# The forget gates' affine steps in the second projection's first pass: from VectorE to ScalarE

## The chip, the cores and the metric

The kernel runs on one core of a Trainium2 chip. The metric is the device time of one execution in microseconds (us), the median of several runs; lower is better. A core has five engines that run their own instruction streams and meet at semaphores: TensorE (PE in the profile; its weight loads are PEld), VectorE (DVE), ScalarE (ACT), GpSimd (POOL) and SyncE (SP), which here only issues DMA transfers.

## The reference, cut to what matters

One inference step of a two-layer encoder: 2048 prompt tokens and 8 x 16 sample tokens, model width 1024, float32. Each layer starts with a projection of the normalized input to 3584 columns:

```python
def rmsnorm(x, g):
    y = x32 * lax.rsqrt(jnp.mean(x32 * x32, axis=-1, keepdims=True) + EPS)
    return (y * g.astype(F32)).astype(x.dtype)

def in_proj(x, g, w):
    p = rmsnorm(x, g) @ w
    m = MIX_WIDTH          # 768
    return (p[..., :m], p[..., m:2 * m], p[..., 2 * m:3 * m],
            heads(p[..., 3 * m:3 * m + X_WIDTH], H_X, HD_X), p[..., 3 * m + X_WIDTH:])
```

In the second layer the second of these blocks, z, gives the forget gates of a gated linear recurrence, and the last block a silu gate:

```python
def hgrn2_inputs(a, b, c, lb):
    z = heads(b, H_B, DK_B).astype(F32)
    lbh = lb.reshape(H_B, DK_B)
    log_f = jnp.logaddexp(jnp.log(lbh), jnp.log1p(-lbh) + jax.nn.log_sigmoid(z))
    k = (1.0 - lbh) * jax.nn.sigmoid(-z)
    return q, k, i, log_f
```

So for each element of z the kernel needs k = (1 - lb) * sigmoid(-z) and f = lb + (1 - lb) * sigmoid(z), with lb one number for each of the 768 channels. Behind the projections come a band attention (layer 0), the recurrence (layer 1), cross-attention and an output projection in each layer.

## The kernel before

The program is a row of stages: an opening, projection 0 (to about 640 us), the band attention, projection 1 (about 1286 to 1910 us), the sample tokens' mixer and the recurrence. A projection is the function `project`. It keeps channels on the partitions: the weight is cut into 28 groups of 128 output channels, taken as 14 pairs ("columns" 0 to 13 in the order of `ORDER`), and the tokens into 4 passes. The first pass is the widest: its tiles are 128x640 in place of 128x512, since it also takes the sample tokens.

One column in one pass is a 2x2 block product done in Strassen's way: 7 products ("steps" or terms 0 to 6). Each step multiplies a sum or difference of weight blocks by one of activation blocks. For float32 accuracy a weight term is split in a high half (L503, ScalarE) and a low half (L510, VectorE), activations too (L395, L399), and a step is 4 matmuls with the low weight half (L1456) and 8 with the high one (L1460). In the first pass the weight sums are made on the spot (L472; terms 0, 1 and 3 on VectorE, 5 and 6 on GpSimd) and SP stores them to DRAM for the later passes (L483). A low half takes the place of its sum in memory, so it waits for that store. SP also stores the finished outputs (L1081, L1086).

The products leave the accumulators so: ScalarE copies steps 0, 1 and 3 into the output tile (`copy`, L1198 and L1201), and VectorE combines steps 2, 3, 4 and 6 into it (`combine`, L1301). The combine of step 2 waits for the copy of step 1, that of step 3 for the copy of step 3 (semaphore `s_cp`).

The order of each engine's instructions is written out by hand as a loop over an iteration number t, at which TensorE is at about step t. In iteration t ScalarE does: copy of step t-1; high half of step t+5; a row of sigmoids, if t is 7q+8 (row 1 of column q) or 7q+9 (row 0); other work by place, such as evacuating transposed activations (L1226). VectorE does: combine of step t-1; the weight sum of step t+6; low half of step t+2; the gates of a row, if t is 7q+9 or 7q+10; other work. SP does: store of the term of step t+4, and for gated columns the output store at t = 7q+13. Engines run in order, so an instruction that waits holds all behind it. TensorE's step needs its low half (`s_lo`).

Columns 3 to 6 are silu gates. Columns 7, 8 and 9 hold the forget gates, in layer 1 only. Their sigmoids and gates are made while the next column multiplies. For each of the two rows (128 channels) of such a column ScalarE's `sigmoid` makes sigmoid(-z) into a second tile (L1212) and sigmoid(z) in place (L1214); VectorE's `gated` multiplies the first by 1 - lb (L1313) and turns the second into lb + (1 - lb) * sigmoid(z) (L1314), and raises `s_post`. The stores wait for `s_post`, and so does the next gated column's sigmoid. In the pieces below, `by_act` does not exist yet.

Of the kernel before, what the change touches and what calls it, by code (L numbers as in the profile page):

```python
# [17 lines left out]
ACT = mybir.ActivationFunctionType  # L18
# [24 lines left out]
GQ, GK, GV, GX, GG = 0, MG, 2 * MG, 3 * MG, 3 * MG + 2  # L43

HALF, SHALF = 2 * P, P // 2
PASSES, TERMS, WPAIRS = NT // 4, 7, NG // 2
STEPS = TERMS * WPAIRS
ORDER = [0, 1, 2] + list(range(GG // 2, NG // 2)) + list(range(3, GG // 2))


def place(step):
    p, r = divmod(step, STEPS)
    c, j = divmod(r, TERMS)
    return p, c, j


def column(q):

    p, c = divmod(q, WPAIRS)
    return WPAIRS - 1 - c if p % 2 else c  # L60
# [21 lines left out]
def wait(eng, sem, value):  # L82

    if not (isinstance(value, int) and value <= 0):
        eng.wait_ge(sem, value)
# [875 lines left out]
def project(nc, l, sem, ps_in, v, x, w, x_of, proj, keep, room, early, samp, opening):  # L961
    ident, g_ln, neg_half = v["ident"], v["g_ln"], v["neg_half"]
    ALL, TILES = PASSES * STEPS, 4 * (PASSES - 1)
    s_cp, s_cb, s_sig, s_post = (sem(f"pj{l}_{n}") for n in ("cp", "cb", "sig", "post"))
    s_mm = w.s_mm
    s_st = samp.s_store if l else opening.s_st
    s_st2 = samp.s_store2 if l else None
# [9 lines left out]
    lb, lb1 = v["lb"], v["lb1"]  # L977
# [6 lines left out]
    plain, gate, forget = "plain", "gate", "forget"  # L984

    def kind_of(q):
        g = 2 * ORDER[column(q)]
        return gate if g >= GG else forget if l and GK <= g < GV else plain
# [6 lines left out]
    def before(q):  # L995

        return sum(2 * each(i) for i in range(q))

    def each(q):
        return COUNT[kind_of(q)]  # L1000

    def rank(q):

        return sum(each(i) > 0 for i in range(q))

    def older(q):

        return max([i for i in range(q) if each(i)], default=0)

    def gates_stored(q, b):  # L1010

        return 16 * sum(1 + 2 * (i < WPAIRS) for i in range(q) if kind_of(i) == forget and rank(i) % 2 == b)

    NOUT, LATER = (3, 13) if l else (2, 11)
# [5 lines left out]
    with ExitStack() as ctx:  # L1020
        ps = ps_in(ctx)
        if room is None:
# [7 lines left out]
        WIDE, nat, out, sig, junk, ss, ms, rs = (  # L1030
            room.WIDE, room.nat, room.out, room.sig, room.junk, room.ss, room.ms, room.rs)

        def sig_of(q):
            return room.sig2[rank(q) % 2] if l else room.last if q // WPAIRS == PASSES - 1 else sig
# [20 lines left out]
        def row_of(q, row):  # L1055
            p = q // WPAIRS
            return slice(0, WIDE) if p == 0 else slice(SHALF, SHALF + 2 * HALF)
# [8 lines left out]
        with nc.Block() as block:  # L1066
            @block.sync
            def _(sp):
                def store(q):
                    p, c = q // WPAIRS, column(q)  # L1070
                    if kind_of(q) == plain:
                        sp.wait_ge(s_cb, 4 * q + 4)
                    else:
                        sp.wait_ge(s_post, before(q) + 2 * each(q))
                    groups = slice(2 * ORDER[c], 2 * ORDER[c] + 2)
                    if kind_of(q) == forget:
                        place_in(v["kgate"][groups.start - GK:groups.stop - GK], sig_of(q), p, s_st2[rank(q) % 2])
                    place_in(proj[groups], out[q % NOUT], p, s_st[q % NOUT])

                def place_in(to, buf, p, s_done):  # L1080
                    sp.dma_start(to[:, :, 2 * HALF * p:2 * HALF * (p + 1)].rearrange("g p n -> p g n"),  # L1081
                                 buf[:, :, SHALF:SHALF + 2 * HALF]).then_inc(s_done, 16)
                    if p == 0:
                        for row in range(2):
                            ends = bass.AP(buf[:].tensor, WIDE * row, [[2 * WIDE, P], [WIDE - SHALF, 2], [1, SHALF]])
                            sp.dma_start(to[row, :, SEQ:NTOK].rearrange("p (h n) -> p h n", h=2), ends).then_inc(s_done, 16)  # L1086
# [60 lines left out]
            @block.gpsimd  # L1147
            def _(pool):
                def load_raw(c):
                    pool.wait_ge(w.s_dve, len(w.ON_DVE) * (c - 1))  # L1150
                    pool.wait_ge(w.s_pool, len(w.ON_POOL) * (c - 1))
                    if TERMS * (c - 2) < w.whole:
                        pool.wait_ge(w.s_mm, TERMS * (c - 2) + 5)
                    else:
                        pool.wait_ge(w.s_lo, TERMS * (c - 2) + 5 - w.whole)
                    for j in w.PLAIN:
                        pool.wait_ge(w.s_tst[j], 16 * (c - 1))
                    pool.dma_start(w.raw[c % 2][:], w.pairs[ORDER[c]]).then_inc(w.s_w[c % 2], 16)

                def load_tile(i):  # L1160
                    if i == 0 and l:
                        pool.wait_ge(s_tp, TURNED)
                    wait(pool, s_tp, TURNED + 2 * (i - 1) if i > 1 else 0)
                    pool.dma_start(nat[i % 2][:], x_of(4 + i)).then_inc(s_in[i % 2], 16)
                if l:
                    early.left(pool, v["s_stx"])
                for j in w.ON_POOL:
                    w.add(nc, pool, j)
                for t in range(ALL):
                    step = t - 1 + TERMS  # L1170
                    if t >= 1 and step < STEPS and step % TERMS in w.ON_POOL:
                        w.add(nc, pool, step)
                    p, c, j = place(t)
                    if l == 0 and (p, c, j) == (PASSES - 1, 4, 0):
                        pool.wait_ge(s_rs, TILES)
                        pool.wait_ge(s_xn, TILES)
                        pool.wait_ge(s_post, before((PASSES - 1) * WPAIRS))
                        opening.blank(nc)
                    if p == 0 and j == 2 and c + 2 < WPAIRS:
                        load_raw(c + 2)  # L1180
                    if p < PASSES - 1:
                        if (c, j) in ((0, 3), (1, 3), (3, 3), (5, 3)):
                            load_tile(4 * p + (c + 1) // 2)
                        if c in (1, 3, 5, 7) and j == 4:
                            i = 4 * p + c // 2
                            pool.wait_ge(s_ms, i + 1)
                            nc.gpsimd.tensor_tensor(rs[:, i:i + 1], ms[:, i:i + 1], neg_half[:, 0:1], ALU.pow).then_inc(s_rs, 1)

            @block.scalar
            def _(act):  # L1190
# [12 lines left out]
                def sigmoid(q, row):  # L1203
                    cols, sig = row_of(q, row), sig_of(q)
                    act.wait_ge(s_cb, 4 * q + 4)
                    wait(act, s_post, before(older(q) if l else q))
                    if l:
                        wait(act, s_st2[rank(q) % 2], gates_stored(q, rank(q) % 2))
                    if kind_of(q) == gate:
                        nc.scalar.activation(sig[:, row, cols], out[q % NOUT][:, row, cols], ACT.Sigmoid).then_inc(s_sig, 1)  # L1210
                    else:
                        nc.scalar.activation(sig[:, row, cols], out[q % NOUT][:, row, cols], ACT.Sigmoid, scale=-1.0).then_inc(s_sig, 1)  # L1212
                        act.wait_ge(s_sig, before(q) + 2 * (1 - row) + 1)
                        nc.scalar.activation(out[q % NOUT][:, row, cols], out[q % NOUT][:, row, cols], ACT.Sigmoid).then_inc(s_sig, 1)  # L1214

                def square(i):
                    act.wait_ge(s_in[i % 2], 16 * (i // 2 + 1))
# [29 lines left out]
                for t in range(ALL + 2 * TERMS):  # L1247
# [12 lines left out]
                    for row, lag in ((1, 8), (0, 9)):  # L1260
                        q, r = divmod(t - lag, TERMS)
# [20 lines left out]
            def _(dve):  # L1282
# [18 lines left out]
                    nc.vector.tensor_tensor(to, to, what, op).then_inc(s_cb, 1)  # L1301

                def gated(q, row):
                    n = before(q) + (1 - row) * each(q)
                    cols, sig = row_of(q, row), sig_of(q)
                    mine = out[q % NOUT][:, row, cols]
                    if kind_of(q) == gate:
                        dve.wait_ge(s_sig, n + 1)
                        nc.vector.tensor_tensor(mine, mine, sig[:, row, cols], ALU.mult).then_inc(s_post, 1)
                    else:  # L1310
                        g = 2 * ORDER[column(q)] + row - GK
                        dve.wait_ge(s_sig, n + 2)
                        nc.vector.tensor_scalar(sig[:, row, cols], sig[:, row, cols], lb1[:, g:g + 1], None, ALU.mult).then_inc(s_post, 1)  # L1313
                        nc.vector.tensor_scalar(mine, mine, lb1[:, g:g + 1], lb[:, g:g + 1], ALU.mult, ALU.add).then_inc(s_post, 1)  # L1314
# [39 lines left out]
                for t in range(ALL + 2 * TERMS):  # L1354
# [15 lines left out]
                    for row, lag in ((1, 9), (0, 10)):  # L1370
                        q, r = divmod(t - lag, TERMS)
# [3 lines left out]
                    if p < PASSES - 1:  # L1375
                        i = 4 * p + c // 2
# [2099 lines left out]
```

## Time and profile before

| | |
|---|---|
| Median of 3 runs | 2385.72 us (2384.73 to 2387.42) |
| Profiled execution | 2395.37 us, its span 2393.6 us |
| Mean granted TensorE clock | 0.993 of full |
| TensorE busy | 2315.6 us (97%) |
| VectorE busy | 1820.2 us (76%) |
| ScalarE busy | 1413.7 us (59%) |
| GpSimd busy | 377.1 us (16%) |
| Projection 1, first pass | about 1286 to 1485 us |
| Projection 1, forget gates of that pass | about 1407 to 1441 us |

The span runs from the first to the last instruction of the profiled execution; the execution's own time is a little longer. Busy shares are means over stages that have different limits. In a timeline row stand the start, the time the instruction or merged run took, the engine, the line of the kernel, and in brackets the idle time before it with what ended it. Neighbouring instructions of an engine overlap a little, so the time it is held is read from start to start.

### The profile page before, as it was taken

Reading aid. Unit: us, or ns where it says so; the run is one execution under the profiler, and the core shown is the slowest. Engines: PE = TensorE matmul, PEld = TensorE weight load, DVE = VectorE, ACT = ScalarE, POOL = GpSimd, SP = SyncE. Lnnn points to the kernel's source line nnn. Section 1 sums busy time; section 2 is a strip of 40 time slices with the busy share of each in tenths; the row PEclk is TensorE's granted clock in tenths of the full one; section 3 lists DMA queues with packets and bytes.
Section 4 is the critical chain, followed back from the end, with each engine's and each line's share of the span. In section 5 each row is a group of like instructions: output and inputs, shape, how many; then the busy total and the mean of one; then the engine's idle time right before and its main releaser. Section 6 shows DMA issues by size and latency. Waiting matters only on the chain. (4 is left out here: it accounts for less than half of the span.)

```text
span 2393.6 us, 61539 instructions
## 1 busy us (share of the span) xinstructions
PE 2315.6 (97%) x23701; PEld 2096.5 (88%) x23701; DVE 1820.2 (76%) x3555; ACT 1413.7 (59%) x3281; POOL 377.1 (16%) x585
## 2 busy tenths in 40 slices
PE   7999999999989999999999999999999989999998
PEld 4999999999967888888887999999999978788886
DVE  7889687887666656666666898797888777788885
ACT  4554666765464555555554564776757566666664
POOL 2322000000012211111112331000000112112111
PEclk9999999999999999999999999999999999999999
DMA  6886987779794222222226887886879793443442
GB/s 218 296 292 224 298 275 227 248 216 329 227 296 143 83 65 83 90 73 83 74 80 226 277 297 242 263 267 213 258 249 310 229 264 108 126 141 121 137 134 70
DMA packets 396664, 469.62 MB, mean 196 GB/s; under 512 B 39861, under 2 KB 248557, under 8 KB 396377
## 3 DMA queue, kind: packets, MB, share of 16 engines
q1 hardware_dynamic: 379832, 406.02, 54.3%
q0 software_dynamic: 14704, 54.92, 6.7%
q10 hardware_dynamic: 1840, 4.75, 0.8%
q8 instruction: 192, 3.15, 0.6%
q14 instruction: 96, 0.78, 0.1%
HBM read 318.77 MB, written 151.56 MB: 196 GB/s over the span
## 5 line engine op out<-in xcount | busy, mean ns | idle before, releaser
L1460 PE MATMUL pj_acc<-x_lo,pj_wh 128*128 128x256 f32 (+1 forms) x3080 | 783.8, 285 | 0.0
L1460 PE MATMUL pj_acc<-x_hi,pj_wh 128*128 128x256 f32 (+1 forms) x3080 | 783.7, 285 | 0.0
L503 ACT ACTIVATE pj_wh<-pj_wt 128x512 fp32r<-128x512 f32 x676 | 420.6, 634 | 270.1 <-DMA pj_wt<-tsum 168.6
L1460 PEld LDWEIGHTS pj_acc<-x_hi,pj_wh 128*128 128x128 f32 x3080 | 579.0, 188 | 0.0
L1460 PEld LDWEIGHTS pj_acc<-x_lo,pj_wh 128*128 128x128 f32 x3080 | 578.7, 188 | 0.0
L510 DVE SCALAR_TENSOR_TENSOR pj_wl<-pj_wt,pj_wh 128x512 fp32r<-128x512 f32 x676 | 467.6, 709 | 93.9 <-ACT pj_wh L503 84.7
L1456 PE MATMUL pj_acc<-x_hi,pj_wl 128*128 128x256 f32 (+1 forms) x3080 | 511.6, 288 | 16.2 <-DVE pj_wl L510 14.1
L1456 PEld LDWEIGHTS pj_acc<-x_hi,pj_wl 128*128 128x128 f32 x3080 | 426.6, 188 | 25.1 <-DVE pj_wl L510 22.4
L1301 DVE TENSOR_TENSOR pj_out<-pj_out,pj_acc 128x512 f32<-128x512 f32 (+1 forms) x448 | 321.2, 717 | 104.5 <-PE pj_acc L1460 71.5
L2526 DVE COPY pb_pt<-pb_SCTP 128x256 f32<-128x256 f32 (+2 forms) x266 | 115.7, 435 | 147.8 <-PE pb_SCTP L2338 74.6
L2661 ACT ACTIVATE pb_se<-pb_se,pb_mn 128x640 f32<-128x640 f32 (+4 forms) x208 | 154.6, 745 | 114.6 <-DVE pb_mn L2509 114.3
L2668 ACT COPY pb_pt<-pb_SCTP 128x384 f32<-128x384 f32 (+2 forms) x272 | 106.3, 391 | 123.6 <-PE pb_SCTP L2342 62.8
L2509 DVE CUSTOM_DVE_ANT_0 pb_se<-pb_SCTP,pb_bias 128x640 f32<-128x640 f32 (+4 forms) x204 | 137.5, 726 | 43.6 <-PE pb_SCTP L2307 39.1
L2338 PE MATMUL pb_SCTP<-ident,pb_se 128*128 128x128 f32 x1020 | 156.9, 276 | 3.9 <-ACT pb_se L2661 2.6
L2338 PEld LDWEIGHTS pb_SCTP<-ident,pb_se 128*128 128x128 f32 x1020 | 121.4, 140 | 38.6 <-issue 9.2
L1198 ACT COPY pj_out<-pj_acc 128x512 f32<-128x512 f32 (+1 forms) x112 | 68.3, 610 | 111.3 <-PE pj_acc L1460 99.2
L1201 ACT COPY pj_out<-pj_acc 128x256 f32<-128x256 f32 (+1 forms) x224 | 85.4, 381 | 72.5 <-PE pj_acc L1460 69.0
L2439 PE MATMUL pb_OP<-pb_woh,pb_yh 128*128 128x512 f32 x264 | 127.1, 482 | 0.0
L3028 PE MATMUL hg_OP<-woh,hg_yh 128*128 128x512 f32 x264 | 116.7, 442 | 2.7 <-issue 2.7
L2216 POOL TENSOR_TENSOR pb_gate<-pb_gate,pb_pt 128x128 f32<-128x128 f32 x136 | 74.9, 550 | 259.3 <-DVE pb_pt L2526 259.3
L2307 PEld LDWEIGHTS pb_SCTP<-pb_k,pb_q 64*128 64x128 f32 x1152 | 86.0, 187 | 24.2 <-issue 11.9
L2307 PE MATMUL pb_SCTP<-pb_k,pb_q 64*128 64x128 f32 (+1 forms) x1152 | 105.3, 329 | 1.8 <-issue 1.8
(361 smaller groups left out, 3966.7 us busy)
## 6 DMA issues: line engine op xcount, KB each, us to landing
pj_wt<-tsum SPq DMA_DIRECT2D x546, 256.0 KB, 3.9
proj<-pj_out SPq DMA_DIRECT2D x112, 512.0 KB, 4.1
tsum<-pj_wt SPq DMA_DIRECT2D x140, 256.0 KB, 3.3
pj_wraw<-in_w_in_dram POOLq DMA_DIRECT2D x24, 1024.0 KB, 6.7
tsum<-pj_wraw SPq DMA_DIRECT2D x56, 256.0 KB, 4.4
hg_x<-x_mid SPq DMA_DIRECT2D x17, 512.0 KB, 3.7
pb_gate<-proj SPq DMA_DIRECT2D x16, 512.0 KB, 5.2
pb_x<-in_x_prompt_dram SPq DMA_DIRECT2D x16, 512.0 KB, 3.6
```

The lines of the kernel that those rows point to most:

```text
L503: nc.scalar.mul(self.hi[j][:], self.source(step), scale_of(column(step // TERMS), self.l)).then_inc(self.s_hi, 1)
L510: nc.vector.scalar_tensor_tensor(out=self.lo[j][:], in0=self.source(step), scalar=scale_of(column(step // TERMS), self.l), in1=self.hi[j][ ...
L1301: nc.vector.tensor_tensor(to, to, what, op).then_inc(s_cb, 1)
L1456: ins = nc.tensor.matmul(BANK[j][:, 0:n], w.lo[j][:, k], x.of(x.hi, p, j)[:, k], start=(k == 0), stop=False)
L1460: ins = nc.tensor.matmul(BANK[j][:, 0:n], w.hi[j][:, k], x.of(y, p, j)[:, k], start=False, stop=(k == 3 and i == 1))
L2307: ins = nc.tensor.matmul(scores_at(u, h, at, size), q[T % 2][po:po + HD, p], kring[po:po + HD, p, slot * P:(slot + size) * P], start=True, ...
L2338: ins = nc.tensor.transpose(to[:, at:at + P], se[u % 2][h][:, i * P:(i + 1) * P], ident[:])
L2439: ins = nc.tensor.matmul(sum_of(job, half), (yl if part == 2 else yh)[job % 2][:, k], (wol if part == 1 else woh)[:, group_of(job, k), cs] ...
L2509: nc.vector.tensor_tensor_reduce(se[u % 2][h][:, 0:n * P], scores_at(u, h, 0, n), add, 1.0, 3e38, ALU.add, ALU.min, mn[:, at:at + 1]).then ...
L2526: ins = nc.vector.tensor_copy(pt[u % 2][h][:, low * P:low * P + width], turned_to(u, h)[:, 512:512 + width])
L2661: nc.scalar.activation(se[u % 2][h][:, 0:n], src, ACT.Exp, bias=mn[:, at:at + 1], scale=-1.0, accum_out=tot[:, at:at + 1]).then_inc(s_exp, 1)
L3028: nc.tensor.matmul(to[:], yh[:, s], woh[:, g, cs], start=(s == 0), stop=False)
```

## The change

Two helper counts and one branch in each place. In the first pass (q < 14), for the forget columns, ScalarE makes both affine steps itself, right behind the row's two sigmoids, and raises a new semaphore `s_aff`; VectorE's `gated` returns at once. SP's store of these columns waits for `s_aff`. What counted `s_post` before now counts only the work that is still VectorE's. The later three passes, and projection 0, keep the old division. Number and size of all transfers stay.

```diff
+    def by_act(q):
+        return kind_of(q) == forget and q < WPAIRS
+    def posts(q):
+        return sum(2 * each(i) for i in range(q) if not by_act(i))
+    def affines(q):
+        return sum(2 * each(i) for i in range(q) if by_act(i))
...
                     if kind_of(q) == plain:
                         sp.wait_ge(s_cb, 4 * q + 4)
+                    elif by_act(q):
+                        sp.wait_ge(s_aff, affines(q) + 2 * each(q))
                     else:
-                        sp.wait_ge(s_post, before(q) + 2 * each(q))
+                        sp.wait_ge(s_post, posts(q) + 2 * each(q))
...
-                    wait(act, s_post, before(older(q) if l else q))
+                    wait(act, s_post, posts(older(q) if l else q))
...
                         nc.scalar.activation(out[q % NOUT][:, row, cols], out[q % NOUT][:, row, cols], ACT.Sigmoid).then_inc(s_sig, 1)
+                        if by_act(q):
+                            affine(q, row)
+
+                def affine(q, row):
+                    cols, sig, mine = row_of(q, row), sig_of(q), out[q % NOUT][:, row, row_of(q, row)]
+                    g = 2 * ORDER[column(q)] + row - GK
+                    nc.scalar.mul(sig[:, row, cols], sig[:, row, cols], lb1[:, g:g + 1]).then_inc(s_aff, 1)
+                    act.wait_ge(s_sig, before(q) + 2 * (1 - row) + 2)
+                    nc.scalar.activation(mine, mine, ACT.Identity, bias=lb[:, g:g + 1], scale=lb1[:, g:g + 1]).then_inc(s_aff, 1)
...
                 def gated(q, row):
+                    if by_act(q):
+                        return
```

## Rows read from the trace of the kernel before

**Rows 1.** The page's first part: busy time, share of the span, instructions

```profile
PE 2315.6 (97%) x23701; PEld 2096.5 (88%) x23701; DVE 1820.2 (76%) x3555; ACT 1413.7 (59%) x3281; POOL 377.1 (16%) x585
```

**Rows 2.** Stretches (columns 8, 9, 10): length, busy time by engine, clock, DMA share

```profile
1404.00:1417.50 13.50, 13.50 (x96) 13.49 (x95) 13.29 (x20) 9.51 (x21) 4.86 (x4) 1.00 0.80 265
1417.50:1430.40 12.90, 12.49 (x87) 12.23 (x85) 12.90 (x20) 9.42 (x17) 4.55 (x4) 1.00 0.99 326
1430.40:1445.80 15.40, 13.04 (x85) 12.44 (x86) 15.40 (x21) 8.89 (x16) 4.14 (x4) 1.00 0.79 265
```

**Rows 3.** TensorE's waits for low halves: group 1404 to 1462; total after 1450

```profile
L1456 PE MATMUL pj_acc<-x_hi,pj_wl 128*128 128x320 f32 x120 | 23.2, 315 | 3.4 <-DVE pj_wl L510 3.4
...
PE pj_acc L1456 <- DVE pj_wl L510: 2.5, 8, 0.7
```

**Rows 4.** Timeline of ScalarE, column 8: start, us, instruction

```profile
1407.38 0.73 ACT L1212 ACTIVATE pj_sig<-pj_out 128x640 f32<-128x640 f32 x1
1408.15 0.74 ACT L1214 ACTIVATE pj_out<-pj_out 128x640 f32<-128x640 f32 x1
1408.79 0.41 ACT L1201 COPY pj_out<-pj_acc 128x320 f32<-128x320 f32 x1
...
1412.56 0.44 ACT L1201 COPY pj_out<-pj_acc 128x320 f32<-128x320 f32 x1
```

**Rows 5.** Timeline of VectorE, column 8

```profile
1409.48 0.55 DVE L1313 TENSOR_SCALAR pj_sig<-pj_sig,lb 128x640 f32<-128x640 f32 x1
1409.94 0.61 DVE L1314 TENSOR_SCALAR pj_out<-pj_out,lb 128x640 f32<-128x640 f32 x1
...
1413.08 0.82 DVE L1301 TENSOR_TENSOR pj_out<-pj_out,pj_acc 128x640 f32<-128x640 f32 x1 [0.21 <-issue]
...
1414.42 0.68 DVE L510 SCALAR_TENSOR_TENSOR pj_wl<-pj_wt,pj_wh 128x512 fp32r<-128x512 f32 x1
```

**Rows 6.** Timeline of TensorE: step 6, columns 8, 9; 0 and 6, column 10

```profile
1415.66 0.83 PE L1456 MATMUL pj_acc<-x_hi,pj_wl 128*128 128x320 f32 x4
...
1428.06 0.75 PE L1456 MATMUL pj_acc<-x_hi,pj_wl 128*128 128x320 f32 x4
1430.39 0.86 PE L1456 MATMUL pj_acc<-x_hi,pj_wl 128*128 128x320 f32 x4 [0.41 <-DVE pj_wl L510]
...
1443.92 0.86 PE L1456 MATMUL pj_acc<-x_hi,pj_wl 128*128 128x320 f32 x4 [1.48 <-DVE pj_wl L510]
```

**Rows 7.** Groups of ScalarE by shape: busy us, mean ns, idle before

```profile
L2661 ACT ACTIVATE pb_se<-pb_se,pb_mn 128x640 f32<-128x640 f32 x144 | 117.9, 820 | 92.6 <-DVE pb_mn L2509 92.6
...
L1210 ACT ACTIVATE pj_sig<-pj_out 128x640 f32<-128x640 f32 x16 | 11.7, 732 | 0.0
...
L1210 ACT ACT_TABLE_LOAD x2 | 2.6, 1283 | 0.0
```

**Rows 8.** Timeline of ScalarE: the copy of step 3, columns 9 and 10

```profile
1424.75 0.42 ACT L1201 COPY pj_out<-pj_acc 128x320 f32<-128x320 f32 x1
...
1438.69 0.41 ACT L1201 COPY pj_out<-pj_acc 128x320 f32<-128x320 f32 x1
```

**Rows 9.** Timeline of VectorE, columns 9 and 10

```profile
1425.48 0.81 DVE L1301 TENSOR_TENSOR pj_out<-pj_out,pj_acc 128x640 f32<-128x640 f32 x1
...
1426.81 0.68 DVE L510 SCALAR_TENSOR_TENSOR pj_wl<-pj_wt,pj_wh 128x512 fp32r<-128x512 f32 x1
...
1429.28 2.75 DVE L510 SCALAR_TENSOR_TENSOR pj_wl<-pj_wt,pj_wh 128x512 fp32r<-128x512 f32 x2
...
1441.26 0.81 DVE L1301 TENSOR_TENSOR pj_out<-pj_out,pj_acc 128x640 f32<-128x640 f32 x1
...
1443.18 0.68 DVE L510 SCALAR_TENSOR_TENSOR pj_wl<-pj_wt,pj_wh 128x512 fp32r<-128x512 f32 x1
```

**Rows 10.** SP's queue, the term stores of column 9; DMA issues, 1400 to 1460

```profile
1419.59 2.41 SPq L483 DMA_DIRECT2D tsum<-pj_wt  x4
...
tsum<-pj_wt SPq DMA_DIRECT2D x23, 256.0 KB, 3.3
```

More of the change, by code:

```diff
@@ L963, in project @@
     ALL, TILES = PASSES * STEPS, 4 * (PASSES - 1)
-    s_cp, s_cb, s_sig, s_post = (sem(f"pj{l}_{n}") for n in ("cp", "cb", "sig", "post"))
+    s_cp, s_cb, s_sig, s_post, s_aff = (sem(f"pj{l}_{n}") for n in ("cp", "cb", "sig", "post", "aff"))
     s_mm = w.s_mm
@@ L1176, in _ @@
                         pool.wait_ge(s_xn, TILES)
-                        pool.wait_ge(s_post, before((PASSES - 1) * WPAIRS))
+                        pool.wait_ge(s_post, posts((PASSES - 1) * WPAIRS))
                         opening.blank(nc)
```

## The prediction, made before the changed kernel had run

> **What bounds the kernel now.** I read the page's first part, then the table of stretches, then the waits, and last the timelines of three engines around the edited lines. TensorE is busy for 97% of the span [rows 1], so a change elsewhere counts only where it lengthens or shortens a TensorE gap. The edited work lies in one place: weight columns 7, 8 and 9 of the second projection's first pass, whose gates are made while the next column multiplies, so in columns 8, 9 and 10, about 1404 to 1446 us. There VectorE is busy 13.29 of 13.50, 12.90 of 12.90 and 15.40 of 15.40 us, ScalarE 9.51, 9.42 and 8.89 [rows 2]. TensorE is short of full by 0.00, 0.41 and 2.36 us in the three [rows 2]; to 1462 it waits 3.4 us in all, every time for VectorE's low halves of the weights, L510 [rows 3]. So VectorE is full and ScalarE has a third free; by totals the edit looks right. The totals do not say where in a column ScalarE's free time lies, and that is the question here.
>
> A column is 7 steps. VectorE's order in it: combine of step 2, low half of step 5, gates, combine of step 3, a weight sum, low half of step 6. The combine of step 3 (L1301) waits for ScalarE's copy of the same step (L1201). TensorE cannot start step 6 without its low half. So a late ScalarE copy of step 3 holds up VectorE and then TensorE. In column 8 ScalarE works without a gap from the first sigmoid at 1407.38 through the copy of step 3, which starts at 1412.56 and ends at 1413.00 [rows 4]; VectorE's combine starts at 1413.08, its low half runs from 1414.42 to 1415.10 [rows 5], and TensorE's step 6 starts at 1415.66 [rows 6]. ScalarE is the chain here already, with 0.56 us to spare at the end.
>
> **The change, part by part.** Removed on VectorE: two instructions for each of 2 rows and 3 columns. They last 0.55 and 0.61 us and overlap their neighbours by about 0.09 (the second starts 0.46 after the first) [rows 5]: 0.46 + 0.52 = 0.98 us a row, 1.96 a column, 5.9 in all.
>
> Added on ScalarE: two activations of 128x640 for each row, one with a per-partition factor, one with a factor and a bias. The trace has none of just this form. A sigmoid of that size holds the engine 0.64 us (1408.15 to 1408.79) [rows 4]. A pointer operand adds 0.09: the exponential of 128x640 with a pointer bias lasts 820 ns, the sigmoid without one 732 [rows 7]. So 0.64 + 0.09 and 0.64 + 0.18, 1.55 us a row, 3.1 a column. Lower bound: no pointer price, 1.28 a row. Upper bound: the second affine also pays what a sigmoid behind an own-engine wait pays (1407.38 to 1408.15 is 0.77, 0.13 more), 1.68 a row. Its new wait is for the sigmoid two instructions back, which ends about 0.65 us before, so I take 1.55. Queued behind it on ScalarE are the copies of steps 1 and 3, the next high halves and the evacuation of transposed activations; the copies have VectorE waiting for them.
>
> Column 8. Both rows' sigmoids precede the copy of step 3 with no gap between, so the whole 3.1 us passes to it: it ends at 16.10 instead of 13.00 (times less 1400). The combine follows 0.08 later, at 16.18; from its start to the end of the low half it was 2.02 us [rows 5], so that half is ready at 18.20 and step 6 starts at 18.23 instead of 15.66: 2.57 us lost. VectorE stands idle for some 4 us before its combine; the 1.96 us it was given are spent there.
>
> Column 9, in times less the shift so far. The copy of step 3 started at 24.75 and lasted 0.42 [rows 8]; now it ends at 28.27, the combine starts at 28.35 instead of 25.48, 2.87 later. The low half of step 6 ended at 27.49 [rows 9] and ends at 30.36; step 6 was to start at 28.06 and loses 2.34. Behind it VectorE goes on without a gap to the next column's first low half, 29.28 [rows 9], which is what releases TensorE at 30.39 [rows 6]. That too moves by 2.87, so column 9 costs 2.87. If GpSimd no longer runs beside that low half, it is 0.4 shorter and the loss 2.5.
>
> Column 10. Before, the copy of step 3 ended at 39.10 and the combine started only at 41.26, since VectorE was behind [rows 8, 9]. Now the copy ends at 42.20 and the combine starts at 42.28, 1.02 later. From the start of the combine to that of the low half took 1.92 here against 1.34 in column 8 [rows 5, 9]. I put this down to a sum on GpSimd beside VectorE's (GpSimd is busy for 4.14 us of this column [rows 2]); with VectorE idle while GpSimd adds, I take the shorter, which gives 0.58 back. So 0.4 is lost. A gap before step 5 may go, but step 6 starts when its low half is there, at 43.92 before, and that decides.
>
> The sum is 2.57 + 2.87 + 0.4 = 5.8 us slower. With 1.28 a row the push is 2.56, and the three cost 2.03, 1.9 to 2.3 and 0: 3.9 at least. With 1.68 it is 3.36: 2.8, 3.1 and 0.7 to 1.3, up to 7.2.
>
> The copies of step 1 are 1.55 us late each. In column 8 that of step 1 ends at 08.79 + 1.55 + 0.41 = 10.75, and the combine of step 2 behind it lies well ahead of the 16.18 above: nothing. The high halves are also late, but by program order each is made three steps before VectorE uses it, over 5 us (column 9 takes 12.9 for seven): nothing, but it would cost if the push passed 5. The stores of the gates now wait for the new semaphore, which ScalarE raises before its copy of step 3, so by 15.7 in column 8; SP comes to them behind the store of the weight sum that follows the combine, after 17.5: nothing. The wait of later sigmoids on the old semaphore counts only gates long finished: nothing.
>
> Two rules of the skill are weighed here. The Trainium skill, Perfetto Trace Analysis, § Optimizing Scalar/DVE Operations: with VectorE saturated, moving work to ScalarE may make sense; rows 2 fit its condition, and by it the gaps of rows 3 would shrink (first rival below). The Trainium skill, ScalarE: Activation LUTs, § Rules for kernel authors, puts multiply and add on VectorE. The rows agree: 1.55 us there for 0.98 here.
>
> **The profile's own time.** The profiled execution took 2395.37 us (span 2393.6 and 1.8 around it), 9.65 above the median of 2385.72. Nothing after 1450 us absorbs a shift by these rows: TensorE's later waits for L510 are 2.5 us in eight pieces, 0.24 of it before 1462 [rows 3]. So the shift passes whole: 2385.7 + 5.8 = 2391.5 us, and a profiled execution of about 2401.
>
> **Rivals.** *VectorE's relief decides (not slower).* The 5.9 us taken from VectorE lie ahead of the L510 instructions that TensorE waits for; if they count, the gaps of 3.4 us close: 2382.3 us. It decides if the copy of step 3 ends before VectorE would reach the combine anyway, 1411.1 in column 8 (13.08 less 1.96). For it speaks that VectorE has no idle time [rows 2]; against it that the copy already ended at 13.00 before anything was added. It could hold in column 10 alone. Chance 0.08.
>
> *Part is given back.* The lag is the same, but TensorE's later waits shrink and the DMA queue, its traffic spread over more time, delivers earlier; at most the 2.5 us of rows 3 are to be had: 2389.0 us. For it: four fifths of the DMA engines' time is used here. Against: those waits follow TensorE's own progress. Chance 0.24.
>
> *Late weight stores add to it.* The weight sum in step 3 is late with the combine, SP stores it before the gates' six transfers, and the term stores queue behind: they were issued from 1419.59 and land 3.3 us later, and VectorE's low halves wait for them [rows 10]. In column 9 the store of step 5 would land at about 1426.2, VectorE wants it at 1427.3: 1.1 us in hand. With a landing of 5 us it costs about 0.6 a column and more in the third: 2393.5 us. Chance 0.06.
>
> *Table switches.* If the affine function is not in the sigmoid's table, each row pays two loads of 1283 ns [rows 7], 5.1 a column on ScalarE and 15.4 in all, nearly all of it on the same chain: 2407 us. The page of the profile shows two loads on L1210, though copies and squares stand between the sigmoids. Chance 0.02. The Trainium skill, ScalarE: Activation LUTs, § Table sets, says that identity lies in every set; the few loads fit that, but no row has the function itself.
>
> **How the numbers follow.** Forecast 0.60, the rivals as given. 0.2% is 4.8 us, about what can be told from no change, so the forecast lies only 1 us above the bound; its own bounds of 3.9 and 7.2 put a seventh of it under. Slower by over 0.2%: 0.51 + 0.06 + 0.02 and a little of the give-back case, 0.60. Faster by over 0.2% needs more than all of VectorE's gaps, 0.04. Same: 0.36. The range: from 2386.8, which takes in most of the give-back case, to 2393.8.
>
> **What would show it.** Right: in columns 8 and 9 ScalarE runs without a gap to the copy of step 3; VectorE idles some 4 us with L1201 as releaser; TensorE has new waits on L510 of about 2.5 us at step 6 of both. The affines last about 0.82 and 0.91 us. Wrong: the combine of step 3 starts with VectorE late rather than ScalarE, or TensorE's waits to 1462 fall below 3.4 us, or the columns after it are shorter than before.

## The result, and the profile after

The changed kernel took 2393.3 us (median of 6 runs, 2391.69 to 2396.56) against 2385.05 of the kernel before (6 runs beside it): a ratio of 1.0035 with a 95% interval of 1.0023 to 1.0047, so 8 us slower, 5.5 to 11.2 by the interval. A second set of runs gave 1.0048 (1.0035 to 1.0060). The forecast was 5.8 us slower, 2391.5 us.

The two profiled executions themselves differ by 1.2 us only (2396.56 and 2395.37). The profile before had reached the second projection 9 us later than the profile after: its first product of that projection starts at 1293.97, the other's at 1284.89, work that the change does not touch. So I compare from that product to the first one of the second pass. That stretch, called the pass below, is 189.94 us before and 199.07 after: 9.1 us longer. From there to the end of the span it is 909.7 us before and 910.8 after; over the twelve profiles of this text that rest varies from 906 to 915 us, so one execution's full time cannot show a change of a few us, and the pass can.

First the stretches of the changed kernel. The columns are those of [rows 2]. The cuts lie at TensorE's step 5 of column 8, step 0 and 1 of column 9, step 6 of column 9, step 1 of column 10, step 6 of column 10, and step 1 of column 11.

```profile
1404.55:1412.16 7.61, 5.49 (x30) 5.02 (x29) 5.02 (x6) 5.73 (x15) 2.56 (x2) 0.84 0.58 194
1412.16:1414.38 2.22, 2.22 (x13) 2.22 (x13) 2.02 (x5) 0.00 (x0) 0.00 (x0) 0.77 1.00 309
1414.38:1425.51 11.13, 8.96 (x63) 8.70 (x61) 5.45 (x10) 9.80 (x17) 2.18 (x2) 1.00 0.71 233
1425.51:1431.08 5.57, 5.18 (x24) 4.78 (x25) 5.57 (x7) 2.16 (x4) 1.29 (x1) 0.69 0.99 309
1431.08:1443.16 12.08, 8.97 (x63) 8.70 (x61) 7.38 (x12) 10.74 (x18) 2.19 (x2) 1.00 0.61 206
1443.16:1448.31 5.15, 5.15 (x25) 5.15 (x25) 5.15 (x6) 1.11 (x3) 1.41 (x1) 0.67 0.98 311
```

VectorE, full before, is now busy for half of the third stretch, and ScalarE for nearly nine tenths of it. New in kind is the granted TensorE clock, the third number from the end of a row: it is 1.00 in all of [rows 2] and here 0.84, 0.77, 0.69 and 0.67 of full in the stretches behind the waits, that is, part of each was run at the lower of the two levels, 1.2 GHz instead of 2.4.

ScalarE in column 8 (timeline; answers to [rows 4], all times some 9 us earlier):

```profile
1398.39 0.73 ACT L1226 ACTIVATE pj_sig<-pj_out 128x640 f32<-128x640 f32 x1
1399.15 0.74 ACT L1228 ACTIVATE pj_out<-pj_out 128x640 f32<-128x640 f32 x1
1399.80 0.82 ACT L1235 ACTIVATE pj_sig<-pj_sig,lb 128x640 f32<-128x640 f32 x1
1400.52 0.91 ACT L1237 ACTIVATE pj_out<-pj_out,lb 128x640 f32<-128x640 f32 x1
1401.33 0.41 ACT L1215 COPY pj_out<-pj_acc 128x320 f32<-128x320 f32 x1
...
1406.62 0.43 ACT L1215 COPY pj_out<-pj_acc 128x320 f32<-128x320 f32 x1
```

The affines hold the engine 0.72 and 0.81 us (1399.80 to 1400.52 to 1401.33), 1.53 a row where I had worked out 1.55. From the first sigmoid to the copy of step 3 it was 5.18 us before and is 8.23.

VectorE in column 8 (answers to [rows 5]), and then the start of the combine of step 3 in columns 9 and 10:

```profile
1399.89 0.68 DVE L510 SCALAR_TENSOR_TENSOR pj_wl<-pj_wraw,pj_wh 128x512 fp32r<-128x512 f32 x1
1401.84 0.82 DVE L1324 TENSOR_TENSOR pj_out<-pj_out,pj_acc 128x640 f32<-128x640 f32 x1 [1.26 <-ACT pj_out L1215]
1402.57 0.69 DVE L510 SCALAR_TENSOR_TENSOR pj_wl<-pj_wt,pj_wh 128x512 fp32r<-128x512 f32 x1
1407.14 0.82 DVE L1324 TENSOR_TENSOR pj_out<-pj_out,pj_acc 128x640 f32<-128x640 f32 x1 [3.88 <-ACT pj_out L1215]
1407.88 0.68 DVE L472 TENSOR_TENSOR pj_wt<-pj_wraw 128x512 f32<-128x512 f32 x1
1408.48 0.68 DVE L510 SCALAR_TENSOR_TENSOR pj_wl<-pj_wt,pj_wh 128x512 fp32r<-128x512 f32 x1
...
1423.43 0.82 DVE L1324 TENSOR_TENSOR pj_out<-pj_out,pj_acc 128x640 f32<-128x640 f32 x1 [2.86 <-PE pj_acc L1485]
...
1441.08 0.82 DVE L1324 TENSOR_TENSOR pj_out<-pj_out,pj_acc 128x640 f32<-128x640 f32 x1 [3.80 <-ACT pj_out L1215]
```

The bracket is the time that VectorE stood before the instruction, with what ended it. It stands 3.9 us for the copy of step 3 in column 8 and 3.8 in column 10. In column 9 the timeline names TensorE for 2.86 us, but the copy it waits for starts at 1422.93 and ends at 1423.33, the combine starts at 1423.43, and TensorE had gone on to step 4 at 1421.42: the named releaser is not the one.

TensorE's first products of a step (answers to [rows 6]): steps 5 and 6 of column 8 with the transposes between them, steps 0 and 1 of column 9; then twice step 6 of a column and steps 0 and 1 of the next.

```profile
1404.55 0.75 PE L1481 MATMUL pj_acc<-x_hi,pj_wl 128*128 128x320 f32 x4
1406.88 0.63 PE L1439 MATMUL pj_tp<-ident,pj_nat 128*128 128x128 f32 x4 [0.41 <-ACT x_raw L1249]
1409.21 1.01 PE L1481 MATMUL pj_acc<-x_hi,pj_wl 128*128 128x320 f32 x4 [1.71 <-DVE pj_wl L510]
1412.16 1.21 PE L1481 MATMUL pj_acc<-x_hi,pj_wl 128*128 128x320 f32 x4
1414.38 0.75 PE L1481 MATMUL pj_acc<-x_hi,pj_wl 128*128 128x320 f32 x4
...
1425.51 0.85 PE L1481 MATMUL pj_acc<-x_hi,pj_wl 128*128 128x320 f32 x4 [2.17 <-DVE pj_wl L510]
1428.39 1.44 PE L1481 MATMUL pj_acc<-x_hi,pj_wl 128*128 128x320 f32 x4 [0.39 <-DVE pj_wl L510]
1431.08 0.75 PE L1481 MATMUL pj_acc<-x_hi,pj_wl 128*128 128x320 f32 x4
...
1443.16 0.85 PE L1481 MATMUL pj_acc<-x_hi,pj_wl 128*128 128x320 f32 x4 [3.11 <-DVE pj_wl L510]
1445.93 1.27 PE L1481 MATMUL pj_acc<-x_hi,pj_wl 128*128 128x320 f32 x4
1448.31 0.75 PE L1481 MATMUL pj_acc<-x_hi,pj_wl 128*128 128x320 f32 x4
```

Each of the three steps starts within 0.1 us of the end of its low half (1409.16 and 1409.21 in column 8). And a step behind a wait is itself long: step 6 of column 8 takes 2.95 us (1409.21 to 1412.16) and step 0 behind it 2.22, where an undisturbed step behind a wait takes 1.87 and a plain one 1.76.

A column's length from its step 0 to the next column's step 0, read from these starts, for all kernels (us):

| kernel | 8 | 9 | 10 | 11 | 12 | pass | pass less before |
|---|---|---|---|---|---|---|---|
| before | 13.19 | 12.89 | 15.40 | 12.97 | 12.83 | 189.94 | |
| after | 16.85 | 16.23 | 17.54 | 12.94 | 12.77 | 199.07 | +9.13 |
| after, again | 15.78 | 15.79 | 18.69 | 12.50 | 12.78 | 198.15 | +8.21 |
| gaps filled | 15.79 | 15.78 | 15.82 | 12.96 | 12.79 | 196.16 | +6.22 |
| push, no relief | 16.95 | 17.53 | 16.06 | 12.96 | 12.79 | 199.03 | +9.09 |
| first affine only | 14.50 | 15.09 | 14.19 | 12.97 | 13.41 | 192.78 | +2.84 |
| copy on VectorE | 13.80 | 14.49 | 13.57 | 12.96 | 13.50 | 191.04 | +1.10 |
| behind the copy | 13.20 | 12.68 | 12.84 | 13.35 | 15.63 | 190.74 | +0.80 |
| behind the copy, again | 13.20 | 12.67 | 12.85 | 16.12 | 12.42 | 190.08 | +0.14 |
| behind the copy, later stores | 13.20 | 12.68 | 12.84 | 13.35 | 12.79 | 187.49 | -2.45 |
| the same, again | 13.20 | 12.67 | 12.84 | 13.36 | 12.79 | 187.53 | -2.41 |
| no affines | 13.19 | 12.68 | 12.83 | 13.36 | 12.77 | 187.42 | -2.52 |

Two of these passes (gaps filled, and the first of behind the copy) hold 0.65 and 0.67 us more in the stretch before column 2, which no edit touches; column 2 is 0.3 us shorter in both.

### The profile page after: what moved, and what is told of

It reads as the page before. It is cut to its first block and busy times, and to the rows that moved or that the text cites. A ratio compares the mean times of both kernels' runs of the same rounds, so it can differ in the third digit from the quotient of the medians.

```text
span 2394.8 us, 61539 instructions
## 1 busy us (share of the span) xinstructions
PE 2314.6 (97%) x23701; PEld 2097.4 (88%) x23701; DVE 1811.7 (76%) x3543; ACT 1425.3 (60%) x3293; POOL 377.6 (16%) x585
## 5 line engine op out<-in xcount | busy, mean ns | idle before, releaser
L510 DVE SCALAR_TENSOR_TENSOR pj_wl<-pj_wt,pj_wh 128x512 fp32r<-128x512 f32 x676 | 465.5, 707 | 83.3 <-ACT pj_wh L503 76.3
L472 POOL TENSOR_TENSOR pj_wt<-pj_wraw 128x512 f32<-128x512 f32 x56 | 86.1, 1539 | 132.5 <-PE pj_acc L1481 97.5
```

The costliest lines, as they stand in the source:

```text
L510: nc.vector.scalar_tensor_tensor(out=self.lo[j][:], in0=self.source(step), scalar=scale_of(column(step // TERMS), self.l), in1=self.hi[j][ ...
```

## The experiments

Two theories stood against each other. Late copy: what counts is how far ScalarE's copy of step 3 is pushed; VectorE's saved time is spent waiting for it, and behind the longer waits TensorE's clock adds to the loss. Load: the work costs on ScalarE wherever it stands, or the loss comes through the stores. A third question is what VectorE's relief is worth by itself.

### The affines behind the copy of step 3

```diff
-                        if by_act(q):
-                            affine(q, row)
...
+                    q, r = divmod(t - 11, TERMS)
+                    if r == 0 and 0 <= q < PASSES * WPAIRS and by_act(q):
+                        affine(q, 1)
+                        affine(q, 0)
```

> The same four affine activations a column stay on ScalarE, but stand behind its copy of step 3 instead of behind each row's sigmoids. Late-copy theory (the loss is the 3.1 us that the affines push ahead of that copy, three times, plus the lower TensorE clock after the stalls): the loss is gone, and VectorE's relief closes most of the 3.4 us of gaps: 2 to 4 us faster than before, no stretch at the lower clock, copy of step 3 with the start it had before. Rival, ScalarE's load counts wherever it stands: still 5 to 8 us slower. Rival, late stores: the stores of the gates start 1.5 us later than in the kernel before, and if the stores were the cause it is slower by 3 or more.

The ratio is 1.0008 (0.9995 to 1.0022), and the pass is 0.80 us longer than before instead of 9.13: nearly all of the loss is gone with ScalarE's load unchanged, so load is out. Columns 8 to 10 are as short as without any affines. But the 2 to 4 us of gain did not come, since column 12 has a new wait of 3.05 us. VectorE's timeline of this kernel shows what lies before it:

```profile
1447.63 0.73 DVE L510 SCALAR_TENSOR_TENSOR pj_wl<-pj_wt,pj_wh 128x512 fp32r<-128x512 f32 x1 [0.31 <-DMA tsum<-pj_wt]
1448.28 1.21 DVE L390 TENSOR_TENSOR x_raw<-x_raw 128x1024 f32<-128x1024 f32 x1
1453.35 0.69 DVE L510 SCALAR_TENSOR_TENSOR pj_wl<-pj_wt,pj_wh 128x512 fp32r<-128x512 f32 x1 [3.86 <-DMA tsum<-pj_wt]
```

A low half waits until the store of its weight sum has landed. The stores of the gates had gone out later in this kernel: SP stood from the term store at 1407.29 to 1409.36 for the affines, which ended at 1409.34, with the next term stores behind.

One thing about the clock shows here. Behind this wait of 3.05 us, as long as any of the changed kernel's, TensorE ran its step in 1.86 us and the granted clock stayed at 1.00:

```profile
1454.10 0.85 PE L1483 MATMUL pj_acc<-x_hi,pj_wl 128*128 128x320 f32 x4 [3.05 <-DVE pj_wl L510]
1455.96 0.75 PE L1483 MATMUL pj_acc<-x_hi,pj_wl 128*128 128x320 f32 x4
```

### Half of the push

```diff
-                    act.wait_ge(s_sig, before(q) + 2 * (1 - row) + 2)
-                    nc.scalar.activation(mine, mine, ACT.Identity, bias=lb[:, g:g + 1], scale=lb1[:, g:g + 1]).then_inc(s_aff, 1)
...
-                    if by_act(q):
-                        return
...
-                        nc.vector.tensor_scalar(sig[:, row, cols], ..., ALU.mult).then_inc(s_post, 1)
+                        if not by_act(q):
+                            nc.vector.tensor_scalar(sig[:, row, cols], ..., ALU.mult).then_inc(s_post, 1)
```

> ScalarE makes only the first affine step (factor 1 - lb), VectorE keeps the second. The push is 0.72 a row, 1.44 a column. Late-copy theory: less the slack of 0.5 in column 8 and 0.2 in column 9, stalls of 0.9, 1.2 and about 0 us, so 2 us slower, and no stretch at the lower clock since the stalls are no longer than those of before: 2 to 3 us slower. Rival, loss in proportion to ScalarE's added time: 3.8 us slower (0.72 of 1.55 of 8.2).

Time 1.0017 (1.0005 to 1.0029), which does not tell 2 to 3 us from 3.8. The pass does: 2.84 us longer. Column 8 is 1.31 longer, 9 is 2.20 longer, 10 is 1.21 shorter. I had expected 0.9, 1.2 and about 0: the sum is right, the two stalls were 0.4 and 1.0 larger, and in column 10 the relief gave back more. Another 0.58 of the 2.84 lies in column 12, which I had not expected. Three tenths of the loss for half of the push: not in proportion. The granted clock is 1.00 from 1396 to 1456, so nothing was lost to it:

```profile
1396.00:1456.00 60.00, 54.55 (x365) 52.98 (x364) 54.39 (x71) 38.73 (x70) 15.98 (x13) 1.00 0.86 278
```

### The push without the relief

```diff
+                        for i in range(2 * (q < WPAIRS)):
+                            nc.scalar.activation(sig[:, row, cols], out[q % NOUT][:, row, cols], ACT.Sigmoid, scale=-1.0).then_inc(s_aff, 1)
+                            act.wait_ge(s_aff, before(q) - before(7) + 2 * (1 - row) + i + 1)
                         nc.scalar.activation(sig[:, row, cols], ..., ACT.Sigmoid, scale=-1.0).then_inc(s_sig, 1)
```

> The kernel before, but ScalarE repeats each first sigmoid of the forget gates twice in the first pass (each behind a wait on itself, 0.77 us: 1.54 us a row, as the affines cost), and VectorE keeps its affine steps. Late-copy theory: the same stalls at step 6 of columns 8 and 9, the relief was worth nothing there; in column 10 VectorE's two steps of 0.98 stand ahead of the same late combine, so nothing either but up to 2 us: 8 to 11 us slower. Rival, the relief did count: 12 us or more slower than before (8.2 plus most of 5.9).

Time 1.0035 (1.0023 to 1.0048), the pass 9.09 us longer, against 9.13 and 8.21 of the changed kernel. In the total, the changed kernel got nothing for the 5.9 us it took from VectorE. But the parts are not the same. Here steps at the lower clock took about 2.1 us more (2.96 and 2.19 in column 8's step 6 and the step behind it, 3.24 and 2.09 around the start of column 10), which leaves about 7.0 us of waits in columns 8 to 10; in the changed kernel the same sum is 3.3 and 5.9. In column 9 the combine of step 3 waited here for VectorE's own gates, 1.04 us past the end of the copy, and step 5 to step 6 took 5.06 us instead of 4.09. So the relief was worth about 1 us of waits, and the clock, which does not fall alike in any two runs, hid it.

### The relief without the push

```diff
-                        if by_act(q):
-                            affine(q, row)
...
-                        sp.wait_ge(s_aff, affines(q) + 2 * each(q))
+                        sp.wait_ge(s_sig, before(q) + 2 * each(q))
```

> Relief without push: in the first pass of the second projection nobody makes the affine steps (the gates of those columns stay plain sigmoids). Late-copy theory: ScalarE is as before and VectorE 1.96 us a column freer: the gaps of column 9 and 10 close, 2 to 4 us faster, none in column 8 where ScalarE was the chain already. Rival, VectorE's load there has no price: within 1 us of before.

The pass is 2.52 us shorter: column 8 unchanged, 9 shorter by 0.21, 10 by 2.57, 11 longer by 0.39. So the relief has a worth where VectorE is behind and nothing is pushed, and it is 2.5 us of the 3.4 in [rows 3]. The timed ratio, 0.9993 (0.9982 to 1.0003), cannot tell that from nothing.

### The waits filled with products

```diff
+    FILL = {8: 8, 9: 9, 10: 11}
...
+                        if l and q in FILL and j == TERMS - 1:
+                            pe.wait_ge(s_cb, 4 * (q - 1) + 4)
+                            for _ in range(FILL[q]):
+                                nc.tensor.matmul(BANK[j][:, 0:P], ident[:], ident[:], start=True, stop=True)
```

> The changed kernel, but TensorE fills most of its three new waits at step 6 (columns 8, 9, 10) with 8, 9 and 11 products of the identity with itself, whose result is overwritten. The late low halves stay as they are. If the 3.3 us above the stalls that I summed come from the lower granted clock behind them: the columns' total is about 5.8 us longer than before instead of 9.1, no step behind a stall takes 2.9 us, and the kernel is 5 to 6 us slower than before (if the fill is shorter than the stall). Rival, the extra time is something else in the late order (weight stores, GpSimd): still 8 to 9 us slower.

The waits are nearly the same in length but filled, up to 0.16 us in column 9 and 0.66 in column 10. TensorE's timeline, column 8 and step 6 of column 9 (L1470 are the fills, each recorded as two):

```profile
1408.77 1.95 PE L1470 MATMUL pj_acc<-ident 128*128 128x128 f32 x16
1410.65 0.85 PE L1486 MATMUL pj_acc<-x_hi,pj_wl 128*128 128x320 f32 x4
1412.52 0.74 PE L1486 MATMUL pj_acc<-x_hi,pj_wl 128*128 128x320 f32 x4
...
1423.07 2.17 PE L1470 MATMUL pj_acc<-ident 128*128 128x128 f32 x18
1425.40 0.86 PE L1486 MATMUL pj_acc<-x_hi,pj_wl 128*128 128x320 f32 x4 [0.16 <-DVE pj_wl L510]
```

Step 6 of column 8 starts 4.68 us after step 5, as late as in the changed kernel (4.66), but then takes 1.87 us instead of 2.95. The stretch from 1396 to 1456, of this kernel and then of the changed one:

```profile
1396.00:1456.00 60.00, 57.52 (x400) 56.26 (x399) 46.44 (x62) 41.98 (x75) 14.62 (x12) 1.00 0.79 257
```

```profile
1396.00:1456.00 60.00, 52.21 (x322) 50.81 (x321) 43.45 (x59) 40.71 (x72) 11.72 (x11) 0.91 0.77 249
```

The pass is 6.22 us longer than before; columns 8 to 12, leaving out what lies ahead of them, are 5.86 longer, against 9.05 in the changed kernel. That is the 5.8 of my sum; the rest of the changed kernel's loss was the clock. Timed it is 1.0021 (1.0008 to 1.0034), beside 1.0048 (1.0035 to 1.0060) of the changed kernel on the same chip.

### The copy of step 3 on VectorE

```diff
-                    if t >= 1 and t - 1 < ALL and (t - 1) % TERMS in (0, 1, 3):
+                    if t >= 1 and t - 1 < ALL and (t - 1) % TERMS in (0, 1, 3) and not mine_too(t - 1):
...
+                    if mine_too(step):
+                        dve.wait_ge(s_cp, 3 * q + 2)
+                        nc.vector.tensor_copy(half(q, 0, 1), BANK[j][:, 0:n]).then_inc(s_cp, 1)
```

> The changed kernel with its affines where it has them, but in columns 8, 9 and 10 VectorE makes the copy of step 3 itself, ahead of its combine. Late-copy theory: the one dependence is cut, so no new wait at step 6 and no lower clock; VectorE is still 1.5 us a column freer than before: 1 to 3 us faster than before. Rival, the loss comes through the high halves, the copy of step 1 or the stores: most of the 8 us stays.

With the affines and all their load in place, cutting this one dependence takes the pass from 9.1 to 1.1 us longer; timed 1.0009 (0.9997 to 1.0020). So the late copy is the cause of the loss, but the 1 to 3 us of gain did not come: two costs stood behind it. In column 8 the low half ends at 1412.06, in good time, yet TensorE starts its transposes late, because ScalarE evacuates the tile before only at 1411.96:

```profile
1413.22 0.63 PE L1446 MATMUL pj_tp<-ident,pj_nat 128*128 128x128 f32 x4 [0.41 <-ACT x_raw L1253]
```

And in columns 9 and 10 the low half of step 6 itself takes 1.82 and 1.81 us instead of 0.68, beside a sum on GpSimd. VectorE, then GpSimd, in column 9:

```profile
1425.18 1.82 DVE L510 SCALAR_TENSOR_TENSOR pj_wl<-pj_wt,pj_wh 128x512 fp32r<-128x512 f32 x1
```

```profile
1425.16 1.28 POOL L472 TENSOR_TENSOR pj_wt<-pj_wraw 128x512 f32<-128x512 f32 x1 [4.05 <-PE pj_acc L1488]
```

### Affines behind the copy, and later stores

```diff
-                    if t >= LATER and (t - LATER) % TERMS == 0 and ... and each(pair(t - LATER)):
+                    if t >= LATER and (t - LATER) % TERMS == 0 and ... and each(pair(t - LATER)) and not by_act(pair(t - LATER)):
                         store(pair(t - LATER))
+                    if t >= LATER + 2 and (t - LATER - 2) % TERMS == 0 and ... and by_act(pair(t - LATER - 2)):
+                        store(pair(t - LATER - 2))
```

> The affines behind the copy of step 3, as in the first experiment, and the stores of the gates two iterations later, so that SP does not stand waiting for the affines (1.8 to 2 us there) with term stores queued behind. If the 3 us wait in column 12 of the first experiment came from that: the first pass is 2.5 to 3 us shorter than before, the kernel 2 to 4 us faster. Rival, that wait was chance in the DMA queue or hangs on the stores being late at all: about no change, as in the first experiment.

> The first experiment's kernel looked at once more, for its 3 us wait in column 12, where VectorE's low half waited for a term store to land. If the wait comes from SP standing still for the affines, it is there again, and the first pass is within 1 us of the kernel before; if it was chance in the DMA queue, it is gone or elsewhere and the first pass is 2 to 3 us shorter than before.

> Affines behind the copy and stores two iterations later, timed again, since five rounds tell 0.1% badly: the first pass 2.4 us shorter than before in the trace as the last time, so 0.9990 by that; if the time does not show it here either, the gain is too small to be told or given back behind the pass.

The kernel without the later stores has its wait again in its second profile. The first row is VectorE's waits for stores from 1400 to 1460 in that profile (total, times, longest), the second TensorE's waits for low halves from 1380 to 1490 in the second profile with later stores:

```profile
DVE pj_wl L510 <- DMA tsum<-pj_wt: 3.9, 1, 3.9
```

```profile
PE pj_acc L1485 <- DVE pj_wl L510: 1.2, 3, 0.8
```

With the later stores the wait is absent both times, and the pass is 2.45 and 2.41 us shorter than before, as without affines at all. So two profiles with and two without speak for the stores and against chance: the wait goes when the gates' stores give way to the term stores. Why it strikes one or two columns after the last forget column, and not in them, I did not trace.

In time this version gave 1.0001 (0.9989 to 1.0013) and 0.9994 (0.9980 to 1.0008), so the 2 to 4 us I expected are not shown. A gain of 2.4 us is 0.1% and neither set of runs tells it from nothing, so it is not a version shown to beat the kernel before. It does beat the changed one: both its intervals end below 1.0023, where the lower of that one's intervals begins.

### The changed kernel again

> The changed kernel once more, beside the other three on one chip: 7 to 9 us slower than before; the first pass of the second projection 9 us longer, of that about 5.8 as waits for the late low half and 3.3 as steps at the lower clock.

Timed 1.0048 (1.0035 to 1.0060), 11 us slower with 8.4 to 14.3 by the interval, where I had expected 7 to 9. The pass is 8.21 us longer. The stalls in columns 8 and 9 are those of the first profile (4.67 and 4.09 us from step 5 to 6), but the lower clock falls elsewhere: step 6 of column 8 takes 1.87 us, step 0 of column 10 takes 3.36, step 1 2.70 and step 6 3.22. Over columns 8 to 10 that is 3.8 us by the clock and 5.0 by waits instead of the 3.3 and 5.8 I had expected; column 10's wait before step 6 is 0.9 shorter, since TensorE comes to it later. From 1430 to 1450 the granted clock is 0.78:

```profile
1396.00:1430.00 34.00, 29.71 (x202) 28.97 (x201) 24.32 (x35) 25.74 (x48) 9.50 (x8) 1.00 0.78 259
1430.00:1450.00 20.00, 17.24 (x91) 16.58 (x91) 14.69 (x20) 13.42 (x22) 4.26 (x4) 0.78 0.73 241
```

## Why the prediction was right, and where it was not

**The price of the affines.** Right: 1.53 us a row for 1.55.

**The push on the copy of step 3.** Right: first sigmoid to copy 8.23 us instead of 5.18 in column 8, 3.05 for 3.1. The copy on VectorE and the affines behind the copy show that this push is the cause: without it 1.1 and 0.8 us of the 9.1 are left.

**Columns 8, 9 and 10.** Expected 2.57, 2.87 and 0.4. From step 5 to step 6 of column 8 it took 4.66 us instead of 2.12: 2.54. In column 9 step 5 to 6 took 4.09 instead of 1.76, 2.33, and step 6 to the next column's step 0 took 2.88 instead of 2.33, 0.55 more: 2.88. Column 10 is 17.54 long; its step 0 and step 6 are long by 0.82 and 0.90 by the clock, which leaves 15.82, 0.42 over before. There VectorE's way from the combine to the low half took 1.34 us (1441.08 to 1442.42), as I had taken it, with GpSimd's sum over by then. The three make 5.84.

**The sum.** "The sum is 2.57 + 2.87 + 0.4 = 5.8 us slower" left out a term. Steps behind the new waits ran partly at the lower clock: 1.08 and 0.46 us in column 8's step 6 and the step behind it, 0.82 and 0.90 in column 10. That is 3.26 us, and with the 5.84 above it is the 9.1 us of the pass. The filled waits show it. The forecast was right in sign and in its mechanism, but its bounds of 3.9 and 7.2 held one mechanism only, and the pass lost more than the upper one. That the time, 2393.3 us, still fell within the range of 2386.8 to 2393.8 is in part luck: it did so by 0.5 us, in a range that nothing had widened for the clock, and the late-stores rival's 2393.5 is met by coincidence.

**"Nothing after 1450 us absorbs a shift."** The pass keeps its 9.1 us, since columns 11 to 13 have their old lengths. The timed difference, 5.5 to 11.2 us, fits that but is too wide to test it.

**The profiled execution.** Forecast about 2401 us, it took 2396.56. I had carried the 9.65 us by which the first profile lay above the median over to the next one; but that profile had already come 9 us late to the second projection, ahead of all that the change touches, so this excess belonged to one execution and not to the kernel.

**The rivals.** Relief: worth something where nothing is pushed (2.5 us, not 3.4), and about 1 us of waits in this order, far under the push; without it the total loss is the same. Late stores: not in the changed kernel, where VectorE waits for no store from 1395 to 1460, but the mechanism is real, as the affines behind the copy showed: there it cost about 3 us. The gain was not given back. No table was switched: the affine activations stand among the sigmoids with 0.72 and 0.81 us from start to start, no room for 1283 ns.

**What I passed over.** ScalarE's evacuation of the transposed tile, which I named as queued and then gave no price: in the changed kernel TensorE's wait of 0.41 us for it is hidden in the longer one, and once that is gone it costs 0.6 us in column 8 (step 5 to 6 takes 2.72 instead of 2.12).

## What to carry to other kernels

A busy share says that an engine is full, not that its neighbour's free time lies where you need it: before moving work, find the instruction of the receiving engine that the others wait for and put the work behind it, not before it. The same four activations in each of three columns cost 8 to 9 us of the pass ahead of one small copy, and behind it, with the stores moved too, nothing against the kernel without them. When a change makes TensorE wait longer, allow for what the steps behind the wait may lose to the clock (here 2.1 to 3.8 us on 5 to 7 us of waits), and when it moves a producer later, look at what stands behind its store in the queue.

## What the runs showed of the hardware

- TensorE's granted clock can fall after a wait on another engine. In columns 8 to 12 of the kernel before no step behind a wait of up to 1.5 us was long; in the changed one waits of 1.7 (with 0.4 just before it), 2.2 and 3.1 us were followed by steps at part of the speed, 0.67 to 0.84 of full over stretches of 2 to 8 us. The same stalls do not always bring it: in the second profile column 8 kept its clock and column 10 lost 0.9 to 1.5 us in each of three steps. Nor does the length of the wait alone decide: in the two profiles with the affines behind the copy, steps behind waits of 3.05 and 2.63 us took 1.86 us, with the clock at 1.00. With identity products in the waits the clock stayed at 1.00 from 1396 to 1456. What else decides stays open.
- A pointer operand costs ScalarE 0.09 us more at 128x640: 0.73, 0.82 and 0.91 us for none, one and two.
- A VectorE low half (L510) took 1.82 us instead of 0.68 beside one GpSimd sum of 1.28 us that started with it, and ended 0.56 us after the sum.
